# Running sums of the decay as triangular products on TensorE, and both turns of a group in the Gram banks, in an RWKV-7 scan

## What is computed

```python
lw = einsum('zbtl,zld->zbtd', tanh(einsum('btd,zdl->zbtl', xw, w1)), w2)   # low-rank product, rank 64
w_raw = -softplus(-(w0 + lw)) - 0.5
decay = exp(-exp(w_raw))              # = exp(-DECAY * sigmoid(w0 + lw)), DECAY = e^-0.5

def _wkv7_step(S, inp):               # one token; S is 64x64 for each head
    sa = S @ aa_t
    S = S * w_t + outer(sa, bb_t) + outer(v_t, k_t)
    return S, S @ r_t
```

## Time and profile before

| | us |
|---|---|
| median of three runs | 5274.54 |
| lowest, highest | 5259.55, 5296.69 |
| the profiled execution: time, span | 5293.9, 5292.1 |
| before the scan (0 to 2487 us of the span) | 2487 |
| the scan, `rwkv_scan` (2487 to 3979) | 1492 |
| behind it (3979 to the end) | 1313 |

### The profile page before, as it was taken

How to read it: one execution, slowest core, us unless ns; L and a number is a source line. 1 busy time by engine, 2 the same in 40 slices (tenths; PEclk the granted TensorE clock), 3 DMA queues, 4 the chain that set the end, 5 groups by cost and what they waited for, 6 DMA issues and landing times. The chain is left out here.

```text
span 5292.1 us, 97295 instructions
## 1 busy us (share of the span) xinstructions
PE 4522.3 (85%) x41944; PEld 3688.9 (70%) x41944; DVE 2327.5 (44%) x4101; ACT 1369.9 (26%) x2742; POOL 1366.0 (26%) x954
## 2 busy tenths in 40 slices
PE   2999798999999969886666777777678899999997
PEld 1788667888888858675555565555564588888886
DVE  3011262351524331431777777777762224243341
ACT  1111273210111123441333333333331121111110
POOL 2111132211111241110544444444431121111110
PEclk6999899999999979897788778778885799999998
DMA  3212333113131222123111111111102221312214
GB/s 121 65 54 75 94 102 101 58 39 117 39 104 50 79 62 77 55 78 90 49 37 47 52 37 52 41 48 47 37 22 92 60 96 36 99 57 67 89 40 162
DMA packets 391574, 360.93 MB, mean 68 GB/s; under 512 B 61264, under 2 KB 358480, under 8 KB 390000
## 3 DMA queue, kind: packets, MB, share of 16 engines
q1 hardware_dynamic: 379312, 344.26, 21.1%
q10 hardware_dynamic: 11840, 10.49, 0.6%
HBM read 252.44 MB, written 102.24 MB: 67 GB/s over the span
## 5 line engine op out<-in xcount | busy, mean ns | idle before, releaser
L422 POOL TENSOR_TENSOR f_wlow<-f_raw,f_whigh 128x1024 fp32r<-128x1024 f32 (+1 forms) x152 | 360.0, 2368 | 1672.4 <-ACT f_whigh L493 1672.4
L478 PE MATMUL f_ps<-fx_hh,f_whigh 128*128 128x512 f32 (+1 forms) x2112 | 530.0, 359 | 0.0
L478 PE MATMUL f_ps<-fx_hl,f_whigh 128*128 128x512 f32 (+1 forms) x2112 | 528.9, 358 | 0.0
L478 PE MATMUL f_ps<-fx_hh,f_wlow 128*128 128x512 f32 (+1 forms) x2112 | 528.0, 358 | 0.0
L493 ACT ACTIVATE f_whigh<-f_raw 128x1024 fp32r<-128x1024 f32 (+1 forms) x152 | 156.6, 1030 | 925.1 <-PE f_ps L478 895.8
L478 PEld LDWEIGHTS f_ps<-fx_hl,f_whigh 128*128 128x128 f32 x2112 | 348.9, 189 | 66.0
L478 PEld LDWEIGHTS f_ps<-fx_hh,f_whigh 128*128 128x128 f32 x2112 | 349.0, 189 | 65.4
L478 PEld LDWEIGHTS f_ps<-fx_hh,f_wlow 128*128 128x128 f32 x2112 | 348.2, 188 | 65.9
L1599 PE MATMUL sc_inv_ps<-sc_tf,sc_bl 64*64 64x64 f32 x6400 | 316.8, 247 | 79.1 <-DVE sc_tf L1940 73.7
L478 PE MATMUL f_ps<-mo_oh,f_whigh 128*128 128x512 f32 (+1 forms) x1440 | 360.4, 359 | 26.7 <-POOL f_wlow L422 26.7
L547 DVE TENSOR_TENSOR f_xo<-f_ps,f_xo 128x512 f32<-128x512 f32 x168 | 90.7, 595 | 618.9 <-PE f_ps L478 586.8
(11 more groups left out here) (263 smaller groups left out, 8915.4 us busy)
## 6 DMA issues: line engine op xcount, KB each, us to landing
f_xo<-xres SPq DMA_DIRECT2D x64, 640.0 KB, 4.1
xres<-f_xo SPq DMA_DIRECT2D x56, 640.0 KB, 2.9
f_raw<-in_ffn_w_gate SPq DMA_DIRECT2D x44, 512.0 KB
f_raw<-in_ffn_w_up SPq DMA_DIRECT2D x44, 512.0 KB
sc_rk<-rkvl SPq DMA_DIRECT2D x80, 256.0 KB, 3.4
rkvl<-ri_ot SPq DMA_DIRECT2D x28, 640.0 KB, 2.9
f_raw<-in_ffn_w_down SPq DMA_DIRECT2D x32, 448.0 KB
qkv_raw<-in_na_w_qkv SPq DMA_DIRECT2D x24, 512.0 KB, 5.5
```

The lines of the kernel that those rows point to most:

```text
L422: nc.gpsimd.tensor_tensor(wlow[:, m % 2, 0:kt], raw[:, 0:kt], whigh[:, m % 2, 0:kt].bitcast(F32), ALU.subtract).then_inc(cut_lo, 1)
L478: last = nc.tensor.matmul(ps[:, m % 2, n, 0:count], w[:, m % 2, k], x[:, k, t0:t0 + count], start=(k == 0 and w is whigh and x is xh), sto ...
```

## The change

The first low-rank product, that of the decay, changes sides. Before, the weights `wa` were stationary and the tokens moved, so that the product had channels on the partitions and the bias w0 came in ScalarE's tanh. Now the tokens are stationary and the weights move, so that it has tokens on the partitions; w0 lies along the free axis and is added by a product of a row of ones with a row of w0, one partition deep, which opens each accumulation. One tanh of 512 columns takes the place of two of 256. `sg` is made right behind the tanhs in s = 0, not in `gates` at s = 1.

`running` (L1552) is new: eight products of `sg` (stationary, 64 tokens by 128 channels) with the triangular mask `m_incl` (64 by 64, moving) write the running sums of both directions into `low_ps` at the end of s = 0, with channels on the partitions. `exps` reads them from there. VectorE's `sums` and the buffers `cum`, `run` and `restart` are gone.

Since `low_ps` now holds the running sums until `exps` has read them, both turns of a group go through `gram_ps`: the first at s = 2 as before, the second at s = 3, once ScalarE has copied the first. The waits of `lora`, `bonus` and `turn` are changed to suit. Two loads of 4 KB (`w0_row`) come in at the start of the scan.

The diff, without declarations and renamed semaphores:

```diff
+        cum_ps = strided(low_ps[:], 0, [[2 * C, Z], [C, U // 2], [512, 2], [1, C]])
...
                 def lora(G):
                     pe.wait_ge(s_in[s], 96 * (G // 2 + 1))
-                    if G >= 3:
-                        pe.wait_ge(a_turn[0], G - 2)
                     if G >= 1:
                         pe.wait_ge(d_bonus, G)
-                    for i in range(2):
+                    for b in range(W // P):
                         for z, rows in enumerate(halves):
-                            last = nc.tensor.matmul(low_ps[:, z, i * W:(i + 1) * W], wa[rows, i, p * P:(p + 1) * P],
-                                                    low[rows, s, i], start=True, stop=True)
+                            nc.tensor.matmul(low_ps[:, z, b * P:(b + 1) * P], one_row[:], w0_row[:, z, p * P:(p + 1) * P],
+                                             start=True, stop=False)
+                            nc.tensor.matmul(low_ps[:, z, b * P:(b + 1) * P], low[rows, s, 0, b * P:(b + 1) * P],
+                                             wa[rows, 0, p * P:(p + 1) * P], start=False, stop=True)
+                    for z, rows in enumerate(halves):
+                        last = nc.tensor.matmul(low_ps[:, z, W:2 * W], wa[rows, 1, p * P:(p + 1) * P],
+                                                low[rows, s, 1], start=True, stop=True)
                     last.then_inc(pe_low, 1)
+
+                def running(G):
+                    pe.wait_ge(a_sg, G + 1)
+                    for b in range(W // P):
+                        for z in range(Z):
+                            for c, rows in enumerate(halves):
+                                last = nc.tensor.matmul(low_ps[:, c, (2 * z + b) * C:(2 * z + b + 1) * C], sg[rows, z, b * P:(b + 1) * P], m_incl[rows, z],
+                                                        start=True, stop=True)
+                    last.then_inc(pe_cum, 1)
...
                 def turn(G, z):
                     if z == 0:
                         pe.wait_ge(v_in[r], 32 * (G // 4 + 1))
-                        if group(G + 2):
-                            pe.wait_ge(a_tanh, G + 3)
-                    elif group(G + 1):
-                        pe.wait_ge(d_gram[1], G + 2)
-                    elif G:
-                        pe.wait_ge(a_turn[1], G)
+                        if group(G + 1):
+                            pe.wait_ge(d_gram[1], G + 2)
+                        elif G:
+                            pe.wait_ge(a_turn[1], G)
+                    else:
+                        pe.wait_ge(a_turn[0], G + 1)
...
                 def bonus(G):
                     pe.wait_ge(d_tb, G + 1)
-                    if G >= 2:
-                        pe.wait_ge(a_turn[0], G - 1)
-                    pe.wait_ge(a_tanh, G + 1)
+                    pe.wait_ge(a_ex1, G + 1)
...
-                        if s == 2 and group(I + 1):
-                            turn(I + 1, 0)
+                        if s >= 2 and group(I + 1):
+                            turn(I + 1, s - 2)
                         inverse(I + 1, 3 * s + 1)
                         if group(I):
                             s_product(I, s)
                         if s < 2 and group(I + 2):
                             gram(I + 2, s)
-                        if s == 2 and group(I + 1):
-                            turn(I + 1, 1)
                         if s == 3 and group(I + 3):
                             bonus(I + 3)
                         inverse(I + 1, 3 * s + 2)
+                        if s == 0 and group(I + 3):
+                            running(I + 3)
...
                 def tanhs(G):
                     act.wait_ge(pe_low, G + 1)
-                    for z in range(Z):
-                        nc.scalar.activation(tw[:, z], low_ps[:, z, 0:W], ACT.Tanh, bias=half_bias[:, z, p:p + 1], scale=0.5)
+                    nc.scalar.activation(tw[:], low_ps[:, :, 0:W], ACT.Tanh, scale=0.5).then_inc(a_tw, 1)
...
+                    act.wait_ge(a_tw, G + 1)
+                    if G >= 1:
+                        act.wait_ge(pe_cum, G)
+                    nc.scalar.activation(sg[:], tw[:], ACT.Identity, bias=consts2[:, 0:1], scale=0.5).then_inc(a_sg, 1)
...
                 def exps(G):
-                    act.wait_ge(d_cum, G + 1)
+                    act.wait_ge(pe_cum, G + 1)
...
-                    nc.scalar.activation(ex2[:], cum[:], ACT.Exp, scale=DECAY).then_inc(a_ex2, 1)
-                    nc.scalar.activation(ex1_of, uc(cum[:]), ACT.Exp, scale=-DECAY).then_inc(a_ex1, 1)
+                    nc.scalar.activation(ex2[:].rearrange("p z (b c n) -> p z b c n", c=2, n=C), cum_ps, ACT.Exp, scale=DECAY).then_inc(a_ex2, 1)
+                    nc.scalar.activation(ex1_pairs, cum_ps, ACT.Exp, scale=-DECAY).then_inc(a_ex1, 1)
...
-                def sums(G):
-                    dve.wait_ge(a_sg, G + 1)
-                    if G >= 1:
-                        dve.wait_ge(a_ex1, G)
-                    nc.vector.tensor_tensor_scan(cum[:, 0], restart[:], sg[:, 0], 0.0, ALU.mult, ALU.add)
-                    nc.vector.tensor_tensor_scan(run[:], restart[:], sg[:, 1], 0.0, ALU.mult, ALU.add).then_inc(d_run, 1)
-                    dve.wait_ge(d_run, G + 1)
-                    back, ahead = (t.rearrange("p (u n) -> p u n", n=C) for t in (cum[:, 1], run[:]))
-                    nc.vector.tensor_copy(back[:, :, 0:1], ahead[:, :, C - 1:C])
-                    nc.vector.tensor_tensor(back[:, :, 1:C], ahead[:, :, C - 1:C].to_broadcast([P, U, C - 1]),
-                                            ahead[:, :, 0:C - 1], ALU.subtract).then_inc(d_cum, 1)
...
-                        if s == 1 and group(I + 3):
-                            sums(I + 3)
```

More of the change, by code:

```diff
@@ L1393, in rwkv_scan @@
         consts2 = ph.sb("consts2", [P, 2])
-        restart = ph.sb("restart", [P, W])
+        one_row = ph.sb("one_row", [1, P])
+        w0_row = ph.sb("w0_row", [1, Z, D])
         wa = ph.sb("wa", [P, 2, D])
@@ L1407, in rwkv_scan @@
         ab = ph.sb("ab", [P, Z, W])
-        cum = ph.sb("cum", [P, Z, W])
-        run = ph.sb("run", [P, W])
         exb = ph.sb("exb", [P, Z, U, C + 1])
@@ L1487, in _ @@
                         sp.dma_start(prm[:, i], q.rearrange("(k p) -> p k", p=P)).then_inc(small_in, 16)
-                for dst, src in loads:
+                for dst, src in loads + [(w0_row[0:1, 0], w0[0:1]), (w0_row[0:1, 1], w0[1:2])]:
                     sp.dma_start(dst, src).then_inc(small_in, 16)
@@ L1531, in _ @@
             def _(pe):
-                pe.wait_ge(small_in, 16 * 15)
+                pe.wait_ge(small_in, 16 * 17)
+                pe.wait_ge(cleared, 1)
                 def lora(G):
@@ L1583, in turn @@
                         for h, rows in enumerate(halves):
-                            last = nc.tensor.matmul(turn_ps[z][halves[1 - h], h, W + s * C:W + (s + 1) * C],
+                            last = nc.tensor.matmul(gram_ps[halves[1 - h], h, W + s * C:W + (s + 1) * C],
                                                     vb[rows, r, z, u * C:(u + 1) * C], ident[rows, rows], start=True, stop=True)
@@ L1717, in _ @@
             def _(act):
-                act.wait_ge(small_in, 16 * 15)
+                act.wait_ge(small_in, 16 * 17)
                 act.wait_ge(params, 1)
-                act.wait_ge(zeroed, 1)
+                act.wait_ge(cleared, 1)
                 def tanhs(G):
@@ L1768, in turn_copy @@
                         act.wait_ge(pe_y, 4 * G - 4)
-                    nc.scalar.activation(t0[:, G % 2, z].rearrange("p h s n -> p h (s n)"), turn_ps[z][:, :, 0:W], ACT.Copy)
+                    nc.scalar.activation(t0[:, G % 2, z].rearrange("p h s n -> p h (s n)"), gram_ps[:, :, 0:W], ACT.Copy)
                     for h in range(2):
                         o = halves[1 - h]
-                        last = nc.scalar.activation(tv[o, G % 2, h, :, z], turn_ps[z][o, h, W:2 * W].rearrange("p (s n) -> p s n", s=U),
+                        last = nc.scalar.activation(tv[o, G % 2, h, :, z], gram_ps[o, h, W:2 * W].rearrange("p (s n) -> p s n", s=U),
                                                     ACT.Copy)
@@ L1793, in _ @@
                             u_copy(4 * I + s)
-                        if s == 3 and group(I + 1):
-                            turn_copy(I + 1, 1)
                         p_copy(I + 1, 3 * s + 1)
@@ L1803, in _ @@
                                 exps(I + 3)
-                        if s == 2 and group(I + 1):
-                            turn_copy(I + 1, 0)
+                        if s >= 2 and group(I + 1):
+                            turn_copy(I + 1, s - 2)
                         p_copy(I + 1, 3 * s + 2)
@@ L2001, in _ @@
             def _(pool):
-                pool.wait_ge(small_in, 16 * 15)
-                pool.wait_ge(zeroed, 1)
+                pool.wait_ge(small_in, 16 * 17)
                 pool.wait_ge(st_cleared, 1)
```

27 lines of the change are left out of this document (10 added, 17 removed).

## The result

| | us |
|---|---|
| median before | 5285.61 (5259.55 to 5296.70, 4 runs) |
| median after | 5419.91 (5414.02 to 5434.00, 4 runs) |
| ratio after / before, with its 95% interval | 1.0265 (1.0217 to 1.0313) |
| span of the profiled execution, before, after | 5292.1, 5421.3 |

I predicted 5197 us, between 5130 and 5280, and gave slower a chance of 0.08. The span of the profiled execution grew by 129 us.

What follows compares the result with a forecast made beforehand. No engine was full, so the prediction took the round of waits between engines as the bound. Its terms summed to -2.1 us a stage, times 37 = -78 us, giving 5197 us from the 5274.5 us median; range 5130 to 5280.

Steps and rivals of the forecast that it cites:

- `sums` leaves the path: End of turn 1: VectorE's `y_out` starts without waiting for the scans, so turn 2's `u_product` comes earlier, -4.35 us a stage.
- The clock comes back in turn 2: From turn 2's `u_product` to turn 3's `x_product`: TensorE's clock recovers without the long idle, -1.0 us, ends 0 and -1.92.
- `lora`: the failed step: Turn 0: `lora`'s burst lengthens by 0.86 to 1.28 us at full clock; +1.4 us with the slow groups counted.
- `running`: Ahead of turn 1's `x_product`: sixteen new instructions, mostly covered by idle time and `gram_out`, +0.2 us, ends 0 and +0.6.
- The lock on `tv`: Turn 1: GpSimd's `kd` comes earlier, `ab` gets between VectorE's two `tv` products, +0.8 us, ends 0 and +1.3.
- the second rival: Turn 1's `tv` products both right behind `kd`, turn 2's clock gain full: -4.1 us a stage, 5122 us, chance 0.2.
- The second turn in turn 3: Between turn 3's `u_product` and `s_product`: the moved turn takes TensorE time, little of it idle, +0.85 us, ends +0.8 and +1.5.
- the slower one: In `lora`, one-row products don't stream because weight loads can't overlap: +1.9 us a stage, 5345 us, chance 0.07.

Runs made afterwards that it cites:

- deep product: Changed kernel with its bias product 64 rows deep (zeros but for one row), in the row half of the product adding to it: 5216.50 us, ratio 0.9855 to before.

## Why the prediction was wrong, item by item

1. **`sums` leaves the path**: right. -4.35 forecast, -4.18 measured (turn 2, x to u).
2. **The clock comes back in turn 2**: wrong, with a size near the forecast by luck. I took -1.0 from turn 2's u to turn 3's x, and these two legs change by -0.10 - 0.67 = -0.77 us. But the granted clock there is 0.51 as in the earlier trace rows, and the -0.67 lies behind `s_product`, where the second turn stood before; I had given its removal nothing of its own. I put the fall of the clock down to the 4.39 us of idle time; with them gone the clock stayed at 0.51. TensorE still idles 1.88 us ahead of turn 2's `x_product`, waiting for the `tv` pair of 2.27 us. With the second turn moved alone, turn 2's leg from u to s stayed at 2.87 us; with GpSimd's order changed too, which brings the pair back to 0.70 us, it fell to 2.13 us and the clock was 1.00 in the stretch shown. Whether GpSimd's order would do it without the second turn moved, no run of the changed kernel shows. The next leg, turn 3's x to u, grew by 0.49 us, and no term of my sum has it. It is not the clock's: it stayed at 4.64 or 4.65 us in every kernel with the change until `y_out` went ahead of `keys` (3.23 us).
3. **`lora`: the failed step.** Forecast +0.86 to +1.28 us at full clock, +1.4 with the share of slow groups; measured +4.86 on its leg. The bounds were both for products that stream, "at worst all in line" included: I took 0.107 us an instruction from rows in which every product has the depth of its neighbours. The one-row product was named as unlike anything in the trace, and then put between rows it wasn't near to. The right price is 0.205 us at 2.4 GHz and 0.36 at 1.2, for each of sixteen instructions. The trace of the kernel before could have warned me: its `y_product` alternates products 64 and 128 rows deep. At full clock two instructions of one depth follow the two before them after 0.05 us once they stream (3262.63 to 3262.69 us, inside the first row below), which would make 0.10 us for four. Each four in alternation take 0.26 us:

```profile
3262.47 0.45 PE L1646 MATMUL sc_chain_ps<-sc_tv,sc_rec 128*64 128x64 f32 x8
3262.85 0.33 PE L1678 MATMUL sc_chain_ps<-sc_rec,sc_st 64*64 64x64 f32 x4
3263.11 0.34 PE L1680 MATMUL sc_chain_ps<-sc_nr,sc_tv 128*64 128x64 f32 x4
3263.37 0.33 PE L1678 MATMUL sc_chain_ps<-sc_rec,sc_st 64*64 64x64 f32 x4
3263.64 0.34 PE L1680 MATMUL sc_chain_ps<-sc_nr,sc_tv 128*64 128x64 f32 x4
```

The Trainium skill's sentence in "TensorE: Matmul & The Clock Gate", Part 2, is that a weight load's time doesn't depend on the row count. The changed kernel's trace agrees: the weight loads of its one-row products take 281 ns in the median, those of the 64-row ones 284. The sentence says nothing of neighbours of another depth, and by leaning on it I passed that by. With a deep product the burst is 1.70 us at full clock, below my lower bound of 1.99, and the leg grows by 0.28 us.
4. **`running`**: +0.2 forecast. In the changed kernel the two legs around it give +2.33 - 1.34 = +1.0 us, with the Gram behind the long `lora` mostly at 1.2 GHz (2.08 us for the earlier trace rows's 1.16). With the deep product they give 1.06 - 1.22 = -0.16 us against before, `lora`'s shift included. But that sum flatters the argument: with `running` moved, 1.2 us went from one leg to the next.
5. **The lock on `tv`**: right. +0.8 forecast, +0.71 measured, with a pair of 2.27 us where "2 us or more" was named. `ab` did go between the two products. The rule of the Trainium skill's "SBUF — State Buffer", "Who interferes with whom", by which the earlier one wins, agrees with that. `ab` starts at 3307.45 us, while the first `tv` product still waits for `kd`, which ends at 3307.49, and the second `tv` product comes behind the first. What failed is what I took the rule to lead to, in item 5 and in the second rival: both `tv` products right behind `kd`. The second of them is never the earlier one.
6. **The second turn in turn 3**: the mechanism right, the size half: +0.85 forecast, +1.43 + 0.48 = +1.9 measured, since it falls at 1.2 GHz (value transposes of 0.80 us and more) and takes `bonus` with it, 2.08 us in every group, where 14 of 40 had the 1.13 of the earlier trace rows before. I had the end +1.5 for it and didn't ask what the clock would be there.

The rival that came true was the slower one, with 0.07. It named the mechanism loosely (weight loads that can't overlap), priced it at 5 us over the old `lora` (measured 4.86 on the leg) and came to +1.9 us a stage; the measured +3.8 differs mainly by item 2, turn 3's +0.49, item 4's +1.0 for +0.6 and item 6's +1.9 for +0.85, for the most part clock.

What shows that item 3 decides is the kernel with the deep product: of my sum's -2.1 us a stage it has -2.0 (36.6 to 34.6), and its 5216.5 us are 81 us under the runs of before beside it. That agreement is partly luck, since item 3 came out 1.1 us below and item 6 1.1 us above, and the smaller misses cancel too.

## What to carry to other kernels

A small product that is folded into a chain of TensorE products should have their depth, filled up with zeros if need be; the rows of zeros add nothing that these runs can show (281 against 284 ns for a weight load of one row and of 64), while a change of depth costs more than a whole product (0.41 us for the two instructions of one, instead of 0.13). When no row shows an operation, bound it by what its neighbours do to it as well as by its own size, and don't call the serial sum of overlapping rates "the worst case". And when GpSimd and VectorE alternate on two-operand instructions, look for the instruction that becomes ready earlier because of the change: it can land ahead of one on the path.

## What the runs showed that I had not expected

- Products of unlike depth (1 and 64, or 32 and 64 rows), in alternation, each follow the other after 0.41 us for two instructions of 128 columns at 2.4 GHz and 0.72 us at 1.2 GHz; of like depth, in both row halves, sixteen of them take 1.0 us. It is so with and without accumulation, and in the same row half or not. Grouping them by depth brought the kernel from 5420 to 5309 us, equal depth to 5217 us. What in the hardware does it these runs don't show. Nor do they show that it is depth alone. Where the depth stays at 64 and the stationary operand goes from 128 to 64 columns, as from the Gram to the inverse in the kernel before, the first instruction starts 0.21 us behind the Gram's last two (3261.63 to 3261.84 us); it may be the operand's whole shape that counts, and no run here varies its columns alone.
- The slow burst costs again through the clock. The first Gram of a group stands behind `lora`; it takes 1.8 us or more in 39 of 40 groups with unlike depths and 1.16 us in 38 of 40 with the deep product. In the steady stretch the mean granted clock was 0.72 with unlike depths, 0.81 with the deep product, 0.83 without a bias product, 0.88 with the two other waits gone (0.80 before).
- GpSimd's and VectorE's two-operand instructions take turns: between two scans, and between two `tv` products, the waiting GpSimd instruction got in, in the stretches shown.
